# The first scales and shifts by products with stationary weights, and the first values, q and k accumulated together

## The reference

```python
c_act = jax.nn.silu(c)                       # one vector of 1024
h = layer_norm(x)                            # x: 512 x 1024
for l in range(DEPTH):                       # DEPTH = 2
    ada = (c_act @ w_ada[l] + b_ada[l])      # 1024 x 6144 weights: shifts, scales and gates
    sh1, sc1, g1, sh2, sc2, g2 = jnp.split(ada, 6, axis=-1)
    u = h * (1.0 + sc1) + sh1
    y = mixer(u, w_in[l], ...)               # u @ w_in: attention q, k, values V, and the mLSTM's parts
    h = layer_norm(DN_ALPHA * h + g1 * y, ...)
    ...
```

## Time and profile before

| | us |
|---|---|
| median of 3 runs (4052.18 to 4057.0) | 4056.42 |
| the profiled execution | 4060.49 |
| its span | 4058.7 |
| TensorE busy | 3738.0 (92%) |
| VectorE busy | 1667.6 (41%) |
| ScalarE busy | 1322.4 (33%) |
| GpSimd busy | 1464.4 (36%) |

### The profile page before, as it was taken

How to read it: one execution, slowest core, us unless ns; L and a number is a source line. 1 busy time by engine, 2 the same in 40 slices (tenths; PEclk the granted TensorE clock), 3 DMA queues, 4 the chain that set the end, 5 groups by cost and what they waited for, 6 DMA issues and landing times. The chain is left out here.

```text
span 4058.7 us, 38874 instructions
## 1 busy us (share of the span) xinstructions
PE 3738.0 (92%) x15948; PEld 2878.6 (71%) x15948; DVE 1667.6 (41%) x2218; ACT 1322.4 (33%) x2140; POOL 1464.4 (36%) x779
## 2 busy tenths in 40 slices
PE   4999888898999999988899899989898999899999
PEld 3887655676888688755577688857467887577887
DVE  5223554436343322455443634344545212374220
ACT  2334234322322234423432232225432222333221
POOL 1232232343455322222234345434124544204543
PEclk9998898999999999989899999999899999899999
DMA  5233211244554323421124355433015333202332
GB/s 176 83 104 104 57 42 35 72 133 120 160 167 134 114 78 94 117 55 42 37 70 132 109 169 168 135 89 90 16 37 148 96 96 91 60 13 87 94 95 77
DMA packets 566895, 385.25 MB, mean 95 GB/s; under 512 B 13518, under 2 KB 504222, under 8 KB 566718
## 3 DMA queue, kind: packets, MB, share of 16 engines
q1 hardware_dynamic: 564494, 379.56, 32.1%
q10 hardware_dynamic: 2224, 3.21, 0.3%
HBM read 379.25 MB, written 2.10 MB: 94 GB/s over the span
## 5 line engine op out<-in xcount | busy, mean ns | idle before, releaser
L144 POOL TENSOR_TENSOR wlo<-raw,whi 128x1024 fp32r<-128x1024 f32 (+2 forms) x538 | 1280.7, 2390 | 2068.2 <-ACT whi L140 2067.8
L174 PE MATMUL ps<-UH,whi 128*128 128x512 f32 x2656 | 1069.7, 403 | 57.8 <-ACT UH L140 36.8
L174 PE MATMUL ps<-UH,wlo 128*128 128x512 f32 x2656 | 1050.4, 395 | 11.3 <-POOL wlo L144 11.2
L174 PE MATMUL ps<-UL,whi 128*128 128x512 f32 x2656 | 1050.2, 395 | 5.1 <-DVE UL L144 3.9
L140 ACT ACTIVATE whi<-raw 128x1024 fp32r<-128x1024 f32 (+2 forms) x538 | 545.8, 1025 | 545.7 <-PE ps L174 253.5
L174 PEld LDWEIGHTS ps<-UH,whi 128*128 128x128 f32 x2656 | 507.6, 191 | 185.2 <-ACT UH L140 43.0
L174 PEld LDWEIGHTS ps<-UH,wlo 128*128 128x128 f32 x2656 | 507.9, 191 | 126.6 <-POOL wlo L144 18.0
L174 PEld LDWEIGHTS ps<-UL,whi 128*128 128x128 f32 x2656 | 506.6, 191 | 123.7 <-DVE UL L144 12.9
L152 DVE SCALAR_TENSOR_TENSOR ACC<-raw,SM,ACC 128x512 f32<-128x512 f32 x336 | 379.6, 1130 | 25.0 <-DMA raw<-in_w_ada 2.8
L174 PE MATMUL ps<-GH,whi 128*128 128x512 f32 x704 | 274.8, 390 | 0.0
L174 PE MATMUL ps<-GL,whi 128*128 128x512 f32 x704 | 274.0, 389 | 0.0
(11 more groups left out here) (295 smaller groups left out, 4442.9 us busy)
## 6 DMA issues: line engine op xcount, KB each, us to landing
raw<-in_w_in SPq DMA_DIRECT2D x170, 512.0 KB, 3.9
raw<-in_w SPq DMA_DIRECT2D x120, 512.0 KB, 5.2
raw<-in_w_ada SPq DMA_DIRECT2D x96, 512.0 KB, 4.9
raw<-in_ada_w SPq DMA_DIRECT2D x96, 512.0 KB, 4.5
raw<-in_ffn_w_gate SPq DMA_DIRECT2D x44, 512.0 KB, 3.9
raw<-in_ffn_w_up SPq DMA_DIRECT2D x44, 512.0 KB, 3.8
raw<-in_ffn_w_down SPq DMA_DIRECT2D x32, 512.0 KB, 3.8
raw<-in_ev_w_in SPq DMA_DIRECT2D x20, 512.0 KB, 4.0
```

The source lines that it names most:

```text
L144: return self.e.tensor_tensor(o, a, b, op).then_inc(*self.done(*keys))
L174: m = self.e.matmul(o, l, r, start=start, stop=stop)
```

## The change

- Units 2 and 0 (the first half of the first scale and of the first shift, FIRST) are no fills any more. Their weights are loaded whole into two new tiles W0, behind x's four row blocks and ahead of all pieces, and TensorE makes them with the weights stationary: 8 x 4 products of a 128 x 128 block with one column of c each, in two rounds. The order of the other units is now FILL: 3, 1, 4, 5, ...
- x is loaded in four parts, centred on VectorE without fills between; one Sqrt for the four blocks.
- ScalarE copies the transposed tiles from PSUM to H; the u tiles are made from H. It splits the first four pieces after two of these copies (up to the second piece of V) and the next four after four UH tiles. ALPHA times H is made later, in the attention's loop.
- Units 3 and 1 are fills between the first u tiles on VectorE, and behind the second and third u tile on TensorE.
- V, q and k of the first pattern are made together in both layers (pe_first): for each u tile the 15 matmuls of V and then 3 of q and 3 of k. q's and k's weights come in halves (4 x 128 rows by 128 columns), so that the pieces are V, q, k, V, V, q, k, V. They use banks 5 and 6.

The diff, cut to its core:

```diff
+    FILL = [3, 1] + list(range(4, 48))
...
     def pe_fill(p):
-        u, n = divmod(fed["fill"], 5)
+        at, n = divmod(fed["fill"], 5)
...
+        u = FILL[at]
...
+        for b in range(4):
+            s.dma(X0[:, b, :], A["x"][0][128 * b:128 * b + 128, :], f"x{b}", "all")
+        for i, q in enumerate(FIRST):
+            for c in range(4):
+                src = A["w_ada"][0][256 * c:256 * c + 256, 512 * q:512 * q + 512].rearrange("(t p) n -> p t n", p=128)
+                s.dma(W0[i][:, 2 * c:2 * c + 2, :], src, f"u{i}{c}", "all")
         for i in range(len(chunks)):
-            if i == NRAW:
-                s.dma(X0[:, :, :], A["x"][0].rearrange("(b p) d -> p b d", p=128), "x", "all")
...
+    FIRST = (2, 0)
+
     def pe_start(p):
         p.wait_ge(*on("const", "all"))
         p.wait_ge(*on("v0", "all"))
-        o = bank(p, AUX, "vt0", ("dve", ("vt", 0)))
+        o = bank(p, (0,), "vt0", ("dve", ("vt", 0)))
         p.tr(o[:, 0:128], rows[:, 0, :], ident, "vt0")
-        for _ in range(20):
-            pe_fill(p)
+        p.wait_ge(*on("act", "cs", 0))
+        for i, q in enumerate(FIRST):
+            os = [bank(p, (0, 1, 2, 3, 4, 5, 6, 7), ("adf", q, m), ("dve", ("adf", q, m))) for m in range(4)]
+            for k in range(NT):
+                p.wait_ge(*on(f"u{i}{k // 2}", "all"))
+                for m in range(4):
+                    p.mm(os[m][:, 0:1], W0[i][:, k, m * 128:(m + 1) * 128], CS[:, k:k + 1], k == 0, k == NT - 1,
+                         *([("adf", q, m)] if k == NT - 1 else []))
         for kt in range(NT):
-            o = bank(p, (0, 1, 2, 3, 4, 5, 6), ("xt", kt), ("act", ("Hs", "n0", kt)))
+            o = bank(p, (0, 1, 2, 3), ("xt", kt), ("act", ("xh", kt)))
...
-        for n in range(20):
-            dve_fill(v)
-            b, part = divmod(n - 7, 3)
-            if not 0 <= b < 4:
-                continue
...
-        wait_ada(v, 0, 0, 1)
-        v.ts(S1, ad(0, 1), 1.0, None, ALU.add, None)
+        for b in range(4):
+            xb, m = X0[:, b, :], ncol[:, b:b + 1]
+            v.wait_ge(*on(f"x{b}", "all"))
...
+        for q in FIRST:
+            for m in range(4):
+                v.wait_ge(*on("pe", "adf", q, m))
+                v.tt(AD[:, 0, 4 * q + m:4 * q + m + 1], ps(("adf", q, m))[:, 0:1], vec("b_ada", 0, 4 * q + m), ALU.add,
+                     ("adf", q, m), ("ad", q))
         sq = norm_tiles("n0")[0]
         for kt in range(NT + 1):
+            if kt == 4:
+                dve_lo(v, "n0", 3, sq)
+                dve_fill(v)
+                v.wait_ge(*on("dve", "ad", 3))
+                v.wait_ge(*on("dve", "ad", 1))
+            if kt in (0, 4):
+                v.wait_ge(*v.prior())
+                v.ts(S1[:, kt:kt + 4], ad(0, 1, kt, 4), 1.0, None, ALU.add, None)
+                v.wait_ge(*v.prior())
             if kt < NT:
                 if kt > 1:
                     v.wait_ge(*on("act", "uh", "n0", kt - 2))
                     v.wait_ge(*on("dve", "ul", "n0", kt - 2))
-                v.wait_ge(*on("pe", "xt", kt))
-                v.ts(sq[kt % 2][:, :], ps(("xt", kt))[:, :], S1[:, kt:kt + 1], ad(0, 0, kt, 1), ALU.mult, ALU.add,
-                     ("s", "n0", kt))
-            if kt:
+                v.wait_ge(*on("act", "xh", kt))
+                v.ts(sq[kt % 2][:, :], H[:, kt, :], S1[:, kt:kt + 1], ad(0, 0, kt, 1), ALU.mult, ALU.add, ("s", "n0", kt))
+            if kt and kt != 4:
                 dve_lo(v, "n0", kt - 1, sq)
+            for _ in range((2, 2, 3, 2, 0, 0, 0, 0, 0)[kt]):
+                dve_fill(v)
...
+        act_warm(a)
         for b in range(4):
-            r = ncol[:, 4 + b:5 + b]
             a.wait_ge(*on("dve", "xc", b))
-            a.af(sqt[:, :], X0[:, b, :], ACT.Square, ("xv", b), accum_out=r)
-            a.wait_ge(*on("dve", "xe", b))
-            a.af(r, r, ACT.Sqrt, ("xs", b))
-        act_split(a, 16 + AHEAD)
+            a.wait_ge(*a.prior())
+            a.af(sqt[:, :], X0[:, b, :], ACT.Square, ("xv", b), accum_out=ncol[:, 4 + b:5 + b])
+        a.wait_ge(*on("dve", "xe"))
+        a.af(ncol[:, 4:8], ncol[:, 4:8], ACT.Sqrt, "xs")
+        for kt in range(NT):
+            a.wait_ge(*on("pe", "xt", kt))
+            a.cp(H[:, kt, :], ps(("xt", kt))[:, :], ("xh", kt))
+            if kt == 1:
+                act_split(a, lin_end["V", 0, 0, "c", 1] + 1)
         sq = norm_tiles("n0")[0]
         for kt in range(NT):
+            if kt == 4:
+                act_split(a, lin_end["V", 0, 0, "c", 3] + 1)
             a.wait_ge(*on("dve", "s", "n0", kt))
             a.cp(UH[:, kt, :], sq[kt % 2][:, :], ("uh", "n0", kt))
-            a.af(H[:, kt, :], ps(("xt", kt))[:, :], ACT.Copy, ("Hs", "n0", kt), scale=ALPHA)
+
+    def act_first_scaled(a, kt):
+
+        a.wait_ge(*on("dve", "s", "n0", kt))
+        a.wait_ge(*on("act", "xh", kt))
+        a.af(H[:, kt, :], H[:, kt, :], ACT.Copy, ("Hs", "n0", kt), scale=ALPHA)
 
     def pool_start(g):
         g.memset(rows[:, :, :], 0.0, "rows")
-        pool_split(g, 16 + AHEAD)
+        pool_split(g, lin_end["V", 0, 0, "c", 3] + 1)
...
+    def pe_first(p, lay, nid):
+
+        bl = v_blocks(0)
+        vb = [bank(p, (0, 1, 2, 3, 4), ("V", lay, 0, i), (v_lane(i), ("VA", lay, 0, i))) for i in range(len(bl))]
+        qb = [bank(p, (5, 6), ("qk", lay, 0, w), ("act", ("qk", lay, 0, w))) for w in range(2)]
+        there = xu(nid)
+        for c in range(4):
+            i = take((True, "w_in", lay, 2 * c, 2, 4112 + 3072, 512))
+            lin_end["V", lay, 0, "c", c] = i
+            if c % 2 == 0:
+                qc = [take((True, "w_in", lay, 2 * c, 4, qk_tile(0, w), 128)) for w in range(2)]
+            for kt in range(2):
+                k = 2 * c + kt
+                p.wait_ge(*there(k)[0])
+                p.wait_ge(*there(k)[1])
+                p.wait_ge(*on("act", "hi", i))
+                p.wait_ge(*on("pool", "lo", i))
+                wh, wl = (x[split_slot(i)][:, kt * 512:(kt + 1) * 512] for x in (his, los))
+                for b, ((cols, m), bk) in enumerate(zip(bl, vb)):
+                    o = bk[0:m, :]
+                    p.mm(o, UH[:, k, cols], wh, k == 0, False)
+                    p.mm(o, UH[:, k, cols], wl, False, False)
+                    ks = ([("used", i)] if kt and b == len(bl) - 1 else []) + ([("V", lay, 0, b)] if k == NT - 1 else [])
+                    p.mm(o, UL[:, k, cols], wh, False, k == NT - 1, *ks)
+                for w in range(2):
+                    j, n = qc[w], k % 4
+                    p.wait_ge(*on("act", "hi", j))
+                    p.wait_ge(*on("pool", "lo", j))
+                    wh, wl = (x[split_slot(j)][:, n * 128:(n + 1) * 128] for x in (his, los))
+                    p.mm(qb[w][:, :], wh, UH[:, k, :], k == 0, False)
+                    p.mm(qb[w][:, :], wl, UH[:, k, :], False, False)
+                    ks = ([("used", j)] if n == 3 else []) + ([("qk", lay, 0, w)] if k == NT - 1 else [])
+                    p.mm(qb[w][:, :], wh, UL[:, k, :], False, k == NT - 1, *ks)
+                    lin_end["qk", lay, 0, w] = j
+                if lay == 0 and k in (1, 2):
+                    for _ in range(5):
+                        pe_fill(p)
...
-        v_rows(0, xu(nid))
+        pe_first(p, lay, nid)
         if lay == 0:
             pe_vectors(p)
-        qk(0, 0)
-        qk(0, 1)
...
-            act_attention(a, lay, (lambda kt: act_scaled(a, "n2", kt, ALPHA)) if lay else None)
+            act_attention(a, lay, (lambda kt: act_scaled(a, "n2", kt, ALPHA)) if lay else (lambda kt: act_first_scaled(a, kt)))
```

More of the change, by code:

```diff
@@ L389, in pe_fill @@
     def pe_fill(p):
-        u, n = divmod(fed["fill"], 5)
+        at, n = divmod(fed["fill"], 5)
         fed["fill"] += 1
-        if u >= 48:
+        if at >= len(FILL):
             return
+        u = FILL[at]
         blk, q = unit_of(u)
@@ L403, in dve_fill @@
     def dve_fill(v):
-        u, n = divmod(fed["dfill"], 5)
+        at, n = divmod(fed["dfill"], 5)
         fed["dfill"] += 1
-        if u >= 48:
+        if at >= len(FILL):
             return
+        u = FILL[at]
         blk, q = unit_of(u)
@@ L411, in dve_fill @@
             v.wait_ge(*landed(i))
-            if u and n == 0:
-                v.wait_ge(*on("pe", "adr", u - 1))
+            if at and n == 0:
+                v.wait_ge(*on("pe", "adr", FILL[at - 1]))
             if n == 0:
@@ L441, in program @@
     sqt = at("sqt", 24, [128, D])
+    W0 = [at(f"W0_{i}", 28 + 16 * i, [128, NT, 512]) for i in range(2)]
     ncol = SM[:, 128:136]
@@ L498, in dve_start @@
         v.cp(VT[:, 0:128], ps("vt0")[:, 0:128], ("vt", 0))
-        for n in range(20):
-            dve_fill(v)
-            b, part = divmod(n - 7, 3)
-            if not 0 <= b < 4:
-                continue
-            xb, m, r = X0[:, b, :], ncol[:, b:b + 1], ncol[:, 4 + b:5 + b]
-            if part == 0:
-                v.wait_ge(*on("x", "all"))
-                v.red(m, xb, ALU.add)
```

(37 more changed lines are left out.)

## The result

The changed kernel takes 4069.42 us as the median of 15 runs (4059.02 to 4071.91); the kernel before, run beside it on the same chip, 4055.55 (15 runs, 4049.38 to 4059.93). The ratio is 1.0029, with a 95% interval from 1.0022 to 1.0036: 8.9 to 14.6 us slower (the two medians alone are 13.9 apart). I had predicted 4067 and 10.3 us slower.

The account below looks back on a forecast made before the run. TensorE's stream plus its gaps was taken to bound the kernel, the largest gap in the first 74.17 us. Losses of 3.1 (first layer) and 7.2 us (second) summed to 10.3 slower, a median of 4067, range 4052 to 4076.

Parts of the forecast that it names:

- Products: First layer's start: the one-column products start at 14.0 us, take 28.8 us and end at 42.8.
- the slow price: First layer's one-column products run at the low clock, 1.8 us for eight.
- V's first matmul: First layer: V starts at 61.8 us, 12.4 us earlier than before.
- The waits: TensorE waits 4.5 us before the first layer's third tile, 3.7 before its fifth, and 5.8 in the second layer.
- The restarts: First layer's stream: two restarts at the low clock behind waits, 1.4 us each, 2.8 in all.
- The second layer: TensorE waits 5.8 us for V's second piece and restarts slowly, 1.4 us: 7.2 us lost.
- What costs nothing: Covered: 42 small loads (15.4 us if uncovered), ALPHA times H in the attention (4.8), second half of x's centring.
- Case 2: First layer: the products raise the clock and take 18.0 us instead of 28.8; -0.5 us, 4056; chance 0.14.
- Case 3: First layer: products keep up with the loads, ending at 25.6; clock holds through waits; -11.1 us, 4045; chance 0.07.
- Case 4: Second layer: V's second piece is ready in time, so no loss there; +3.1 us, 4060; chance 0.07.
- Case 5: VectorE's fills and tiles queue behind GpSimd's rests; further waits of 2 to 4 us; +16 to +22; chance 0.15.
- first layer's, 3.1: First layer loses 3.1 us: 12.4 gained by V's earlier start, minus 15.5 for waits, restarts, reducings and tail.

Follow-up runs that it names:

- experiment 3: Changed kernel plus five unread 512-column warming matmuls on TensorE ahead of the one-column products: 4062.87 us, ratio 1.0030.
- Experiment 1: Changed kernel with unit 3 reduced behind the first u tile instead of the second: 4062.01 us, ratio 1.0031.
- the second kernel of experiment 7: Mended first layer, old second-layer order, plus V's third piece split ahead of the fifth UH tile and three others ahead of the sixth: 4041.92 us, ratio 0.9964.
- experiment 2: Changed kernel with four pieces instead of three, V's second among them, split ahead of the second layer's norm: 4065.19 us, ratio 1.0035.
- second trace: Changed kernel, unedited, run again for another trace: 4067.68 us, ratio 1.0032.
- experiment 6: Changed kernel with old second-layer order: 4061.78 us, ratio 1.0024; kernel before with only the new second-layer order: 4061.8 us, ratio 1.0024.

## Why the prediction was right

The sign, the size and the two places of the loss were right. That the sum comes so near is in part luck, as the steps show:

- **Products.** Start 14.20 (14.0 predicted), 27.4 us for the 128 (28.8). They ran at 1.71 us for eight; the slow price held, and in experiment 3 the clock fell under them. The granted clock of 14.20 to 41.60 reads 1.00 in the trace of after, at the same pace (4.7 instructions a us) that reads 0.50 in experiment 3. Going by durations and not by that record was the right choice of the two. The Trainium skill (TensorE: Matmul & The Clock Gate, table "Why this matters for your kernels") asks for TensorE kept busy; in experiment 3 it was, for 19 us of these products at a granted clock of 0.50 without a rise, so for them the measurement decides against the rule.
- **V's first matmul.** 62.80 (61.8). Here two errors cancel in part: the three rests on GpSimd ended at 50.79 (52.3 predicted), but the load behind them, issued at 50.82, was waited for till 57.10, 6.3 us where I had taken 3.9 from the earlier trace rows. The 3.9 is a median over the whole kernel; here one load had been issued 1.7 us before it, and two more followed within 0.9.
- **The waits.** Before the third tile 4.18 (4.5), before the fifth 3.26 (3.7), in the second layer 5.45 (5.8). Each place was as named. The trace gives ScalarE's UH for the first two where I had said VectorE's UL. Before the third tile they end 0.1 us apart, the UH last; before the fifth the UL is the later one, as I had said: it ends at 95.75, and V goes on at 95.85. Experiment 1, the second kernel of experiment 7 and experiment 2 each took one of the three waits away by its cause alone.
- **The restarts.** This is the step that was off: "1.4 more for each start at the low clock", and two of them. In the first trace 11, 13 and, behind the vectors, 8 matmuls were slow (2.2, 2.6 and some 1.6 us); in the second 9, none and 6 (1.8, 0, 1.2). So there are three and not two, since TensorE also stands 2.05 us before the vectors, and each costs from nothing to 2.6. V's start itself, where I had taken 7 slow ones for both kernels, had 11 and 8 in the changed kernel and 6 and 12 in the one before. qk(1, 0) starts at 121.20 and at 117.00 where I had 118.3, and by the mark the first layer lost 7.3 us in the first trace and 2.8 in the second, against 3.1: the size of this term is right only as a middle of such draws.
- **The second layer.** 7.6 us by the stretch (7.2), and 6 to 14 by experiment 6.
- **What costs nothing.** SP issued the small loads from 85.28 to 100.46, 22 to 38 us into the stream (20 to 36), and none of TensorE's waits is put down to them. That nothing was lost behind the mark, where ALPHA times H now stands, shows at TensorE's first gap of over a us there. It is 251.8 us behind the mark in both kernels, with the same wait, before and then after:

```profile
372.51 0.66 PE L178 MATMUL ps<-CO,sx 128*128 128x128 f32 x4 [1.77 <-ACT sx L136]
```

```profile
380.40 0.66 PE L178 MATMUL ps<-CO,sx 128*128 128x128 f32 x4 [1.77 <-ACT sx L136]
```

- **The rivals.** Case 2 falls with experiment 3. Case 3 falls with the products' 27.4 us. Case 4 falls: the wait is there, in all six traces whose second layer has the new order without the further piece of experiment 2. Case 5 wanted two or three more waits between the tiles; there are the two forecast, and no third.

The sum of 10.3 lies in the measured 8.9 to 14.6; the marks of the two traces give 14.9 and 10.4. The mechanism held in every place named. The size of the second layer's part is well founded. That of the first layer's, 3.1, is near one trace (2.8) and less than half of the other (7.3), and is right by luck as much as by working.

## What to carry to other kernels

Ask of each gap put into a full TensorE stream what piece, slot or scale its next tile waits for, and put the splits, reducings and loads in the order in which the stream wants them: with the same new start the kernel is 12 us slower or 21 us faster than before, by the order of a few splits and one reducing and by the order of accumulation. A reordering made for one layer, with a gap to fill, should not be given to a layer that has none: it only moved V's second piece behind q's and k's. And try the parts of a change apart: the interleaving looked like the heart of this one, and its gain was in the start.

## What the hardware showed that I had not expected

- The one-column products did not hold a high clock that TensorE already had: after ten instructions of 512 columns they ran at 9 to 10 instructions a us for 4 us, and then at 4.8 at a granted clock of 0.50, with no idle time between.
- The granted clock reads 1.00 for the first products of an execution in which TensorE has done nothing else, at the pace that elsewhere reads 0.50. There the durations say more.
- The same wait of 3.26 us in the same program was followed by 13 slow matmuls in one execution and by none in another. The Trainium skill (TensorE: Matmul & The Clock Gate, part 1) says that the number of slow matmuls at a kernel's start varies from run to run (6, 11 or 14 in one kernel). That page speaks of the start of a kernel; behind this wait in the middle of one, where eight traces have it, the number is 0 to 14. The 15 timed runs of the changed kernel go with it: those with a mean granted clock of 0.952 took 4059 to 4061 us, those with 0.948 or 0.949 took 4069 to 4072. So a price of a restart from one trace is one draw, and two spans of single executions can agree by chance while the medians are 14 us apart.
- Taking one wait of 4.18 us away moved the mark by 9.1 us, one of 3.25 by 7.1. In the first case the wait and the 11 slow matmuls behind it are 6.4 of it; the rest is an earlier V (0.9) and fewer slow matmuls at the other starts (7 for 11 and 8 for 13). Against the second trace of the changed kernel the same edit is worth 4.7. A step told by one trace on either side carries such draws.
